# A two-block transformer layer on one core: other banks, orders and pieces in the second mixer

## The reference, cut to what matters

```python
h = rms_norm(x, ln1_g)
z_a, z_b, z_c, z_g = split(h @ w_in, [2*512, 2*512, 3*512])
u, v = split(gelu(z_a), 2)
y_a = (u * chunked_spatial_gating(layer_norm(v), sg_w, sg_b)) @ w_a_out
p, g_lin = split(z_b, 2)
c = causal_depthwise_conv(p * sigmoid(g_lin), cv_w, cv_b)        # 31 taps
y_b = silu(layer_norm(c)) @ w_b_out
q, k, vv = split(z_c, 3)                                          # 8 heads of 64, q and k normalised
y_c = stick_breaking_attention(q, k, vv) @ w_c_out
gates = sigmoid(z_g + b_gate)                                     # three gates of 1024
x = x + (gates[0]*y_a + gates[1]*y_b + gates[2]*y_c) @ w_out
h2 = rms_norm(x, ln2_g)
up = causal_depthwise_conv(h2 @ w_up, ffn_conv_w, ffn_conv_b)     # 3 taps
gate, val = split(up, 2)
x = x + (silu(gate) * val) @ w_down
```

## Time and profile before

| | |
|---|---|
| median of 3 runs | 797.46 us (794.4 to 797.86) |
| the profiled execution | 796.17 us, span 794.4 us |
| TensorE busy | 753.3 us, 95% of the span |
| VectorE busy | 554.4 us, 70% |
| ScalarE busy | 371.4 us, 47% |
| GpSimd busy | 12.7 us, 2% |
| mean granted TensorE clock | 0.983 of full speed |
| HBM read | 150.45 MB, 191 GB/s over the span |

### The profile page before, as it was taken

How to read it: one execution, slowest core, us unless ns; L and a number is a source line. 1 busy time by engine, 2 the same in 40 slices (tenths; PEclk the granted TensorE clock), 3 DMA queues, 4 the chain that set the end, 5 groups by cost and what they waited for, 6 DMA issues and landing times.

```text
span 794.4 us, 13306 instructions
## 1 busy us (share of the span) xinstructions
PE 753.3 (95%) x5388; PEld 708.6 (89%) x5388; DVE 554.4 (70%) x774; ACT 371.4 (47%) x463; POOL 12.7 (2%) x27
## 2 busy tenths in 40 slices
PE   4899979799999999999999999899998999999998
PEld 3789968699999888889979899898998999999998
DVE  4879887576565844457899976737857888887441
ACT  4124352464545232366654546555446554644330
POOL 0000000000000000020000101000000000000000
PEclk9899998899999999999999999999999999999999
DMA  9999795254565995436445342335653455533640
GB/s 316 349 376 333 242 354 212 106 207 165 183 188 184 314 285 176 153 123 221 162 156 189 120 146 106 120 120 173 238 197 122 159 178 193 165 140 115 213 137 27
DMA packets 52927, 152.17 MB, mean 192 GB/s; under 512 B 2640, under 2 KB 33488, under 8 KB 42512
## 3 DMA queue, kind: packets, MB, share of 16 engines
q1 hardware_dynamic: 52512, 150.20, 54.7%
q0 software_dynamic: 368, 1.31, 0.5%
HBM read 150.45 MB, written 1.05 MB: 191 GB/s over the span
## 4 chain that ended last, share of the span: by engine, by line
PE 74%; DVE 12%; ACT 5%; SPq 3%; issue 3%; DMA 2%; ACTq 0%; DVEq 0%
PE ps L1335 17%; PE ps L1333 16%; PE ps L1334 16%; PE ps L1457 5%; PE ps L1459 5%; PE ps L1458 5%; DVE w_lo L853 4%; SPq L375 2%; DVE cacc L1167 2%; DVE ada_acc L857 2%; ACT w_hi L491 2%; PE ps L1391 1%; DMA raw<-in_w_sc_in 1%; PE ps L1475 1%; DMA raw<-in_ada 1%
## 5 line engine op out<-in xcount | busy, mean ns | idle before, releaser
L853 DVE TENSOR_TENSOR w_lo<-raw,w_hi 128x2048 fp32r<-128x2048 f32 (+2 forms) x120 | 255.1, 2128 | 104.5 <-ACT w_hi L491 104.4
L1333 PE MATMUL ps<-a_hi,w_hi 128*128 128x256 f32 x1072 | 305.1, 285 | 0.8 <-DVE w_lo L853 0.7
L1335 PE MATMUL ps<-a_hi,w_lo 128*128 128x256 f32 x1072 | 302.9, 283 | 0.0
L1334 PE MATMUL ps<-a_lo,w_hi 128*128 128x256 f32 x1072 | 300.9, 281 | 0.0
L491 ACT ACTIVATE w_hi<-raw 128x2048 fp32r<-128x2048 f32 (+2 forms) x120 | 213.3, 1781 | 111.7 <-PE ps L1459 46.2
L1334 PEld LDWEIGHTS ps<-a_lo,w_hi 128*128 128x128 f32 x1072 | 203.3, 190 | 0.6 <-issue 0.5
L1333 PEld LDWEIGHTS ps<-a_hi,w_hi 128*128 128x128 f32 x1072 | 201.3, 188 | 2.7 <-issue 1.7
L1335 PEld LDWEIGHTS ps<-a_hi,w_lo 128*128 128x128 f32 x1072 | 201.0, 187 | 0.0
L857 DVE SCALAR_TENSOR_TENSOR ada_acc<-raw,silu_c,ada_acc 128x256 f32<-128x256 f32 (+1 forms) x77 | 53.5, 702 | 2.7
L1457 PE MATMUL ps<-w_hi,hid_hi 128*128 128x512 f32 x128 | 50.9, 398 | 0.0
L1459 PE MATMUL ps<-w_hi,hid_lo 128*128 128x512 f32 x128 | 50.7, 396 | 0.0
(11 more groups left out here) (231 smaller groups left out, 916.3 us busy)
## 6 DMA issues: line engine op xcount, KB each, us to landing
raw<-in_w_z_in SPq DMA_DIRECT2D x26, 1024.0 KB, 4.7
raw<-in_w_up SPq DMA_DIRECT2D x22, 1024.0 KB, 4.7
raw<-in_w_mlp_in SPq DMA_DIRECT2D x16, 1024.0 KB, 4.8
raw<-in_w_mlp_out SPq DMA_DIRECT2D x16, 1024.0 KB, 5.7
raw<-in_w_down SPq DMA_DIRECT2D x16, 704.0 KB, 4.1
raw<-in_ada SPq DMA_DIRECT2D x16, 512.0 KB, 8.9
raw<-in_ada_half SPq DMA_DIRECT2D x8, 1024.0 KB, 6.6
raw<-in_ada SPq DMA_DIRECT2D x8, 1024.0 KB, 5.2
```

The source lines that it names most:

```text
L853: e.tensor_tensor(w_lo[:, slot, 0:words], raw[:, unit_slot, 0:words], w_hi[:, slot, 0:words].bitcast(f32), SUB).then_inc(raw_used, 1)
L1333: e.matmul(dst, w_hi[:, slot, cols], hi, start=start, stop=False, skip_group_check=skip)
L1334: e.matmul(dst, w_hi[:, slot, cols], lo, start=False, stop=False, skip_group_check=skip)
L1335: return e.matmul(dst, w_lo[:, slot, cols], hi, start=False, stop=stop, skip_group_check=skip)
```

## The change

Five edits: v goes to banks 6 and 7, and the branch and output products use their banks in another order; at the gating step VectorE does the gating before that step's low part; the first 18 gate tiles get their sigmoid in two pieces of 9 behind steps 23 and 24, the last 6 get it on their way out of PSUM; the convolution's squares come before the gates of step 22 on ScalarE; and the last norm's squares and sums follow the output product block by block.

```diff
+        MIX_BANK = [2, 3, 0, 1]
 # ScalarE
-            def x_norm(norm, shift):
...
+                if s == CV_VAR_STEP:
+                    for t in range(2):
+                        e.wait_ge(cv_cent, 2 * t + 2)
+                        square(SQ["cv"] + t, flat(cacc[:, 2 * t:2 * t + 2, :]))
                 if kind in ("q", "k", "pg", "u", "gate"):
                     e.wait_ge(w_used, g + 1 + USED)
...
-                        e.activation(vg[:, c, :], ps[:, TOKEN_BANK + c, :], ACT.Gelu_apprx_tanh).then_inc(vg_ready, 1)
+                        e.activation(vg[:, c, :], ps[:, SG_BANK + c, :], ACT.Gelu_apprx_tanh).then_inc(vg_ready, 1)
...
                 if kind == "gate":
                     for h in range(2):
                         n = 2 * (s - Z_ORDER.index("gate")) + h
-                        ins = e.activation(gates[:, n, :], ps[:, bank, h * T:(h + 1) * T], ACT.Identity,
+                        late = s > CV_VAR_STEP
+                        ins = e.activation(gates[:, n, :], ps[:, bank, h * T:(h + 1) * T], ACT.Sigmoid if late else ACT.Identity,
                                            bias=pcol("b_gate", n))
-                        ch.mark(ins) if h == 0 else ins.then_inc(z_free_act, 1)
+                        if h == 1:
+                            ins.then_inc(z_free_act, 1)
+                        elif late:
+                            ins.then_inc(gates_late, 1)
+                        else:
+                            ch.mark(ins)
+                    if CV_VAR_STEP < s <= CV_VAR_STEP + 2:
+                        part = s - CV_VAR_STEP - 1
+                        if part == 0:
+                            e.wait_ge(z_free_act, 11)
+                            ch.wait()
+                        wide = flat(gates[:, 9 * part:9 * part + 9, :])
+                        e.activation(wide, wide, ACT.Sigmoid).then_inc(gates_ready, 1)
...
                 if s == CV_VAR_STEP:
-                    for t in range(2):
-                        e.wait_ge(cv_cent, 2 * t + 2)
-                        square(SQ["cv"] + t, flat(cacc[:, 2 * t:2 * t + 2, :]))
                     inverse_rms(STATN["cv"], SQ["cv"] + 2, T, SG)
...
-            e.wait_ge(z_free_act, 14)
-            ch.wait()
-            e.activation(flat(gates[:, 0:6, :]), flat(gates[:, 0:6, :]), ACT.Sigmoid).then_inc(gates_ready, 1)
-            e.activation(flat(gates[:, 6:24, :]), flat(gates[:, 6:24, :]), ACT.Sigmoid).then_inc(gates_ready, 1)
...
             for j in range(N_BLOCKS["mix_out"]):
                 high_at(FIRST["mix_out"] + j + AHEAD)
-            x_norm("ln2", None)
+                if j:
+                    e.wait_ge(x_new, 2 * j)
+                    square(SQ["ln2"] + j - 1, flat(x[:, 2 * j - 2:2 * j, :]))
+            e.wait_ge(x_new, DT)
+            square(SQ["ln2"] + 3, flat(x[:, 6:8, :]))
+            inverse_rms(STATN["ln2"], SQ["ln2"] + 4, T, D)
+            act_high("ln2", None)
 # VectorE
-                ahead_at(g + AHEAD)
+                if s != SG_STEP:
+                    ahead_at(g + AHEAD)
...
                         split(br["a"][0][:, t, :], br["a"][1][:, t, :], o, br_a)
+                    ahead_at(g + AHEAD)
...
-                e.wait_ge(gates_ready, 1 if j < 2 else 2)
+                e.wait_ge(gates_ready, 1 if j < 3 else 2)
+                if j == 6:
+                    e.wait_ge(gates_late, 3)
+                    e.wait_ge(z_free_act, 14)
...
-                bk = 2 * (j % 2)
+                bk = 2 - 2 * (j % 2)
...
-                e.tensor_tensor(pair, pair, ps[:, j, :], ADD).then_inc(x_new, 2)
+                e.tensor_tensor(pair, pair, ps[:, MIX_BANK[j], :], ADD).then_inc(x_new, 2)
 # TensorE
-                e.wait_ge(vg_ready, 2)
+                e.wait_ge(vv_ready, 2)
...
-                    if kind == "v" and first:
-                        e.wait_ge(vv_ready, 2)
-                    token_block(s, 0 if first else 4)
+                    token_block(s, 0 if first else 4, SG_BANK if kind == "v" else TOKEN_BANK)
...
-                            mm = product(half(2 * (b % 2) + n // 2, n % 2), (g0 + b) % SPLIT_SLOTS, 4 * n + k,
+                            mm = product(half(2 - 2 * (b % 2) + n // 2, n % 2), (g0 + b) % SPLIT_SLOTS, 4 * n + k,
...
-            first_block(mix_ready, 0, raw_unit(g0) + 1, g0, 0, a_hi, a_lo)
+            first_block(mix_ready, 0, raw_unit(g0) + 1, g0, MIX_BANK[0], a_hi, a_lo)
             for j in range(1, 4):
-                pair_block(raw_unit(g0 + j) + 1, g0 + j, j, a_hi, a_lo)
-            x_norm("ln2")
+                pair_block(raw_unit(g0 + j) + 1, g0 + j, MIX_BANK[j], a_hi, a_lo)
+                sum_squares(SQ["ln2"] + j - 1, STATN["ln2"], j == 1, False)
+            sum_squares(SQ["ln2"] + 3, STATN["ln2"], False, True)
```

More of the change, by code:

```diff
@@ L304, in build_program @@
         gates_ready = sem("gates_ready")
+        gates_late = sem("gates_late")
         mix_sum = sem("mix_sum")
@@ L1518, in _ @@
             turn("post", 1, x_t)
-            def x_norm(norm):
-                for t in range(4):
-                    sum_squares(SQ[norm] + t, STATN[norm], t == 0, t == 3)
             g0 = FIRST["mlp_in"]
@@ L1587, in _, with token_block @@
             g0 = FIRST["z_in"]
-            def token_block(j, k0):
+            def token_block(j, k0, first_bank):
                 e.wait_ge(raw_used, raw_unit(g0 + j) + 1)
@@ L1593, in token_block @@
                 for c in range(2):
-                    dst, tok = ps[:, TOKEN_BANK + c, :], slice(c * P, (c + 1) * P)
+                    dst, tok = ps[:, first_bank + c, :], slice(c * P, (c + 1) * P)
                     for k in range(k0, k0 + 4):
```

## The result

The changed kernel takes 793.02 us (median of 11 runs, 791.12 to 796.11), the kernel before 797.51 (11 runs, 794.4 to 799.74): 0.9942 of the time, 95% interval 0.9927 to 0.9956, 4.5 us. The profiled execution took 792.01, its span is 790.2.

A forecast was written before the change was run, and what follows sets the result against it. TensorE, busy 95% of the span, was taken as the bound. The terms summed to -6.1, +1.5 for low clock made -4.6: 791.6 against the profiled execution, 792.9 against the median; forecast 792.0 us, range 789.3 to 795.2 (8 in 10).

The forecast's parts named there:

- v banks: Second mixer, v into banks 6 and 7: TensorE's wait for vv goes and VectorE moves earlier too, -1.4 us.
- Gating order: Gating step: the 1.7 gained at branch a is given back waiting for the taps, 0 (bounds 0 and -1.7).
- Squares: Convolution's variance: squares ahead of gates on ScalarE remove TensorE's wait, -1.7 us (bounds -1.4 and -1.8).
- Branch stage: Sigmoids in pieces: the mixing wait goes (2.1 with margins) and the low clock behind it, -3.6 us (bounds -2.1, -3.8).
- Exchanged branch banks: Branch stage: the 1.3 wait for the last gates stays, as TensorE's wait for the fourteenth eviction does; 0 (bounds +0.3, -0.1).
- Last norm: Sums by block: 1.0 less from addition to root, 1.6 for two sums on TensorE's path; +0.6 us (+0.2 to +1.0).
- The sign that I had named for a wrong term: A shorter stretch from the output product's last block to the up projection would show the last norm's +0.6 wrong-signed.
- The low clock at the longer wait: One low-clock stretch, more likely than not, at the mean's wait grown to 2.2 us or around the norm: +1.5 us.
- -6.1: Sum in us of the edits' terms over the second mixer and last norm, before +1.5 for the clock.
- Rival 1: No new low clock behind the waits: the whole -6.1 stands, 790.1 to 791.4 us; chance 0.22.
- Rivals 2 and 3: Tap chain not binding: 788.5 to 790, chance 0.06; branch-stage wait or low clock stays, or squares late: 793.5 to 795, 0.22.
- rival 4: Slower: TensorE idles in several places, each low stretch costs 1.5, the fifth further makes it slower; 797.5 to 803, chance 0.05.

## Why the prediction was right, step by step

The time, the range and the sign were right (792.0 said, 793.02 measured). The working was right in the waits and wrong in the clock, in two places that cancelled; that they cancelled was luck.

- v banks, -1.4: 1.43 at the gating mark, and in the edit alone VectorE ended its taps 1.44 earlier. In the change it ended them only 1.24 earlier. The 0.2 belongs to the gating order, which loses it alone too: there and in the change VectorE's first multiplication by u takes 0.61 instead of 0.43, and why it does stays open (before, then after):

```profile
448.77 0.43 DVE L1228 TENSOR_TENSOR sgo<-sgo,u_sb 128x256 f32<-128x256 f32 x1
```
```profile
447.24 0.61 DVE L1238 TENSOR_TENSOR sgo<-sgo,u_sb 128x256 f32<-128x256 f32 x1
```

- Gating order, 0: shown twice, by the wait for the taps of 2.4 (2.2 said) in the change and in the edit alone, and from the other side by moving the taps, after which the same order is worth 1.7. That VectorE and ScalarE had a loop of their own was the step that decided it.
- Squares, -1.7: 1.8 in the edit alone and in the change.
- Branch stage, -3.6: the wait of 1.93 went (2.1 with its margins, as said). The other 1.5 were the low clock behind it (1.8 measured), and the kernel does not always have that: in its second execution it isn't there and the stage takes 36.2 instead of 38.0. A term of the sum was read from one execution of something that comes and goes.
- Exchanged branch banks, 0: the wait for the gates stayed 1.3, and went when TensorE's wait was moved. So that part of the change had no effect on this wait, as argued.
- Last norm, +0.6: +0.7, with both halves as worked out (1.0 saved, 1.7 spent for 1.6). The sign that I had named for a wrong term doesn't tell: with two sums moved ahead of it, the last block lies nearer to the up projection (VectorE's last addition starts 4.68 ahead of it instead of 5.68), and the edit costs 0.7 all the same.
- The low clock at the longer wait, +1.5: there in one of five executions with that wait, not in the two profiled ones of the changed kernel. The rows of three shorter waits without one were taken as a sign that length decides; 1.6 us was enough in two other executions and 2.4 not enough in four.

Without any low stretch the two kernels stand at 191.28 and 186.56, 4.7 apart; the medians are 4.5 apart (3.5 to 5.8 by the interval). My -6.1 took one low stretch too many from before, and +1.5 gave one too many to after; -4.6 came out near both by that. Which low stretches the runs without a profile had is not known. The two profiled executions of the kernel before (796.17 and 795.79) were faster than its median, so its usual run may well have more of them than these two show. Rival 1, no new low clock, is what both profiles after show, and its -6.1 is the 6.2 of the profiled stretch; its time (790.1 to 791.4) was missed, since part of the -6.1 was low clock that comes and goes. Rivals 2 and 3 didn't occur, and rival 4 needed five low stretches where at most two were seen in one execution of the second mixer.

The Trainium skill, "TensorE: Matmul & The Clock Gate", section "Part 1: The HAM clock gate (the "warmup" mystery)", says of the start of a kernel that the number of slow matmuls there is not the same from run to run. The traces show the like in the middle of one: the same wait of the same program had a low stretch in one execution and none in another.

The Trainium skill, "TensorE: Matmul & The Clock Gate", section "Why this matters for your kernels", warns only of idle gaps longer than any here. The traces disagree: four kinds of wait of 1.6 to 2.4 us had low stretches behind them, 9 times in 29.

## What to carry to other kernels

Before a wait is credited, follow the waited-for engine to the next place where the bottleneck needs it: an order swap on an engine that runs its own loop moves the wait and removes nothing, until its loop is shortened. Price what a low clock behind a wait costs as a chance, from several executions of each version, and not as part of the wait. When sums or other small work are moved ahead, ask whether they lay beside someone else's work where they were.

## What was not expected of the hardware

- The granted clock fell behind waits as short as 1.6 us, and didn't in other executions with waits of 2.4. One low stretch cost 1.5 to 1.8 us. Behind the norm this can be read from the time from the up projection to the end: 194.9 to 195.0 us in the ten executions without one, 196.4 to 196.5 in three with one, and 197.6 in the one with two pieces (12 and 18 matmuls in 3.4 us each), 2.7 more.
- Two programs with the same first 400 us reach the second vv step up to 3.8 us apart (406.27 to 410.07), more than most edits here are worth. The marks inside one stretch repeat to 0.02 us.
- Fourteen extra products of 128x256 in a 2.1 us wait left the following marks where they were (181.60 and 181.56).
